# Moving the prompt's group merge into the sample attention of a hybrid decoder step

## The reference, cut to what matters

```
def merge_groups(outs, lses):
    wts = jax.nn.softmax(jnp.stack(lses, 0), axis=0)
    o = jnp.sum(wts[..., None] * jnp.stack(outs, 0), axis=0)
    return o.reshape(o.shape[0], o.shape[1], B_HEADS * HEAD_DIM)

o = jnp.concatenate([o_a, o_b], axis=-1)      # 512 sparse + 256 merged columns
y = jnp.einsum('bte,ed->btd', o, w_out)       # output projection, 768 -> 1024
```

## Time and profile before

| | |
|---|---|
| median of 3 executions | 2952.39 us (2942.93, 2952.39, 2952.66) |
| the profiled execution | 2945.84 us |
| its span, first to last instruction | 2944.0 us |
| mean granted clock of TensorE over the span | 0.946 of 2.4 GHz |
| sample attention | 820.72 to 869.80 us of the span |
| merge | 869.80 to 919.98 |
| output projection, to its last matmul | 919.98 to 997.70 |

### The profile page before, as it was taken

The page is one execution under the profiler, slowest core; times in us unless marked ns, Lnnn a source line. Parts: engine busy times, 40 slices in busy tenths (PEclk is TensorE's granted clock), DMA queues, the critical chain, the costliest instruction groups (busy, mean ns, idle before and its releaser), DMA issues. The chain is left out here.

```text
span 2944.0 us, 39798 instructions
## 1 busy us (share of the span) xinstructions
PE 2691.4 (91%) x15960; PEld 2492.5 (85%) x15960; DVE 1259.2 (43%) x2222; ACT 645.1 (22%) x1148; POOL 959.2 (33%) x466
## 2 busy tenths in 40 slices
PE   6789998778855899999999998996999999999999
PEld 5557877765634899999999997895989999999999
DVE  5157888667725422222222235566342222222222
ACT  4242221546522201000110022345120010001100
POOL 3013440005613533323333344332333333233323
PEclk8889999868966999999999998998999999999999
DMA  4121222524144111111111111223111111111112
GB/s 137 70 59 60 90 77 76 188 69 121 40 140 151 46 49 43 43 43 43 43 43 43 49 43 54 69 91 140 38 38 44 48 45 43 43 43 43 43 43 83
DMA packets 109909, 196.50 MB, mean 67 GB/s; under 512 B 24205, under 2 KB 66317, under 8 KB 109517
## 3 DMA queue, kind: packets, MB, share of 16 engines
q1 hardware_dynamic: 109794, 194.97, 20.7%
HBM read 169.92 MB, written 46.06 MB: 73 GB/s over the span
## 5 line engine op out<-in xcount | busy, mean ns | idle before, releaser
L2014 POOL TENSOR_TENSOR unit_low<-unit_raw,unit_high 128x1024 fp32r<-128x1024 f32 x160 | 450.2, 2814 | 1238.0 <-DVE unit_high L2010 1237.4
L2306 DVE TENSOR_TENSOR x_t<-x_t,m_ps 128x1092 f32<-128x1092 f32 x128 | 165.4, 1292 | 522.9 <-PE m_ps L2027 522.9
L2027 PE MATMUL m_ps<-m_hidden_high,unit_high 128*128 128x364 f32 x1536 | 341.4, 330 | 3.1 <-POOL m_hidden_low L2213 2.9
L2027 PE MATMUL m_ps<-m_hidden_high,unit_low 128*128 128x364 f32 x1536 | 339.6, 329 | 0.0
L2027 PE MATMUL m_ps<-xg_high,unit_high 128*128 128x364 f32 x1536 | 339.3, 329 | 0.0
L2027 PE MATMUL m_ps<-xg_low,unit_high 128*128 128x364 f32 x1536 | 338.8, 328 | 0.0
L2027 PE MATMUL m_ps<-m_hidden_low,unit_high 128*128 128x364 f32 x1536 | 338.4, 328 | 0.0
L2027 PE MATMUL m_ps<-xg_high,unit_low 128*128 128x364 f32 x1536 | 338.0, 328 | 0.0
L2240 ACT ACTIVATE m_relu<-m_ps 128x1092 f32<-128x1092 f32 x64 | 69.4, 1084 | 1210.3 <-PE m_ps L2027 1210.3
L2294 DVE TENSOR_TENSOR m_relu<-m_relu,rstd_all 128x1092 f32<-128x1092 f32 x64 | 83.0, 1296 | 583.5 <-ACT m_relu L2240 583.4
L2027 PEld LDWEIGHTS m_ps<-m_hidden_high,unit_high 128*128 128x128 f32 x1536 | 265.4, 188 | 12.0 <-POOL m_hidden_low L2213 7.9
(11 more groups left out here) (331 smaller groups left out, 3839.9 us busy)
## 6 DMA issues: line engine op xcount, KB each, us to landing
unit_raw<-w_units SPq DMA_DIRECT2D x160, 512.0 KB, 3.5
w_raw<-w_in SPq DMA_DIRECT2D x48, 256.0 KB, 2.9
proj_rows<-rows SPq DMA_DIRECT2D x32, 256.0 KB, 2.0
s_win<-win_cache SPq DMA_DIRECT2D x2, 3968.0 KB
sw_rows<-proj_rows SPq DMA_DIRECT2D x16, 384.0 KB, 3.5
proj_rows<-rows SPq DMA_DIRECT2D x36, 128.0 KB, 1.8
select_work<-xt SPq DMA_DIRECT2D x8, 546.0 KB, 3.7
x_t<-xt SPq DMA_DIRECT2D x4, 1092.0 KB, 11.6
```

Source lines behind the costliest of these rows:

```text
L2014: self.nc.gpsimd.tensor_tensor(self.wl[slot][:, :], self.raw[:, slot, :], self.wh[slot][:, :].bitcast(F32), ALU.subtract).then_inc(self.w_ ...
L2027: last = self.nc.tensor.matmul(ps[:, c, 0:CH], w[wslot][:, wk], v[:, k, c, :], start=(k == 0 and n == 0), stop=(k == nk - 1 and n == 2))
L2306: nc.vector.tensor_tensor(d.x[:, n, :, :], d.x[:, n, :, :], ps[s][:, :, 0:CH], ALU.add).then_inc(d.taken[s], 1)
```

## The change

The merge stage is gone. Its work on the prompt's 8 tiles is now done in the sample attention, one tile a step beside the items; its work on the 64 own rows is done in the output projection.

- **Sparse attention**: after the last page keys, SP loads the window rows of four tiles (`MERGE_FIRST`) into the part of `work` that is free by then.
- **Sample attention**: SP loads a fifth tile ahead of the windows and three behind them. The sums (`merge_below`, `merge_shares`) run for 5 and 3 tiles at a time in steps 1, 2, 6 and 7, the shared products in steps 2 to 9, the adds on POOL, the transposes in steps 4 to 11. ACT copies each turned tile and stores it to `mixed` blocks 4 and 5, and it also stores the items' rows, which are now kept by head (64 outputs, maximum, sum: 66 words). `ob` has 5 buffers instead of 3; the new values have 2 slots instead of 3.
- **Output projection**: SP loads two units, then the own rows (8 + 12 loads), then the parameters and the trunk. ACT's queue loads the six blocks of `mixed`; ACT copies the high parts, DVE makes the low ones. PE makes chunks 1 and 2 (columns 364 on) of the first two units block by block as they come, then turns the own rows, then makes chunk 0, which holds the 64 own columns. The second unit's low part is made by DVE.

The own rows' loads:

```
 class OwnRows:
-    LOADS = AH + NG * BH * 3
+    LOADS = AH + NG * BH
...
+            src = bass.AP(tensor=self.obs.tensor, offset=base + h * (DT * OBW + HD + 2), ap=[[32 * OBW, DB], [OBW, DT], [1, HD + 2]])
+            sp.dma_start(self.b[0:TS, g, h, :], src).then_inc(self.all_in, 16)
```

In `stage_sparse`, on SP, behind the loads of tile j:

```
+                if j == LAST_J - 1:
+                    sp.wait_ge(masked, len([t for t in MASKED if ITEMS[t][0] < LAST_J]))
+                    for n in range(MERGE_FIRST):
+                        smp.load_merge(sp, obp, smp.rows_a[:, n, :, :], n)
```

In `stage_sample`, on SP:

```
+            load_new(1)
+            load_new(0)
+            for n in range(MERGE_FIRST, 5):
+                smp.load_merge(sp, obp, merge_rows(n), n)
             for x, (_, g, i) in enumerate(rest):
                 smp.load_window(sp, a, g, i, kb[x + 2], vb[x + 2], win_in[x + 2])
...
+            for n in range(5, NM):
+                smp.load_merge(sp, obp, merge_rows(n), n)
```

In `stage_sample`, on ACT, at the end of step t:

```
+                n = t - 5
+                if 0 <= n < NM:
+                    act.wait_ge(m_turned, n + 1)
+                    if n >= NMO:
+                        act.wait_ge(m_out[n % NMO], 16 * (n // NMO))
+                    nc.scalar.activation(mt[:, n % NMO, :, :], psx[n % 2][:, 0:2 * P].rearrange("p (k n) -> p k n", k=2), ACT.Copy
+                                         ).then_inc(m_taken, 1)
+                if t >= 3:
+                    store_item(t - 3)
+                if 0 <= n < NM:
+                    store_merge(n)
```

In `stage_sample`, on PE, at the end of step t:

```
+                if t >= 4:
+                    turn_merged(t - 4)
```

In `stage_sample`, on DVE, at the end of step t:

```
+                if t in (1, 6):
+                    merge_below((1, 6).index(t))
+                if t in (2, 7):
+                    merge_shares((2, 7).index(t))
+                if 2 <= t < NM + 2:
+                    merge_rows_of(t - 2)
```

In `stage_out_projection`, on ACT:

```
+            for k in range(NK):
+                act.dma_start(raw[:, k, rows], mixed[k][:, rows]).then_inc(mixed_in[k], 16)
+            for k in range(NK):
+                act.wait_ge(mixed_in[k], 16)
+                nc.scalar.activation(oh[:, k, rows], raw[:, k, rows], ACT.Copy).then_inc(high, 1)
```

In `stage_out_projection`, on PE:

```
+            pe.wait_ge(d.w_low, 2)
+            pe.wait_ge(cleared, 2)
+            for k in range(NK):
+                pe.wait_ge(low, k + 1)
+                for u in range(2):
+                    d.part_product(pe, ps[u], u, k, NK, oth, otl, (1, 2))
+            pe.wait_ge(own.all_in, OWN)
+            pe.wait_ge(merged, 1)
...
+            pe.wait_ge(own_low, 1)
+            for u in range(2):
+                for k in range(NK):
+                    last = d.part_product(pe, ps[u], u, k, NK, oth, otl, (0,))
+                last.then_inc(d.made, 1)
```

More of the change, by code:

```diff
@@ L169, in build_program @@
             otl = c1.enter_context(nc.sbuf_tensor("mixed_low", [P, 6, NCH, CH], F32R))
[L170 to L172 removed]
+            stage_out_projection(nc, a, d, ident, mixed, own, oth, otl)
         stage_mlp(nc, a, d, 0, 0)
@@ L175, in build_program, with released, runs_of @@
         stage_mlp(nc, a, d, 1, 2, o["y_t"])
+def released(nc, known):
+    return sorted(int(s) for s in nc.released_uncleared_semaphores if int(s) not in known)
+def runs_of(numbers):
+    out = []
+    for n in numbers:
+        if out and n == sum(out[-1]):
+            out[-1] = (out[-1][0], out[-1][1] + 1)
+        else:
+            out.append((n, 1))
+    return out
 class Select:
@@ L986, in _ @@
         def _(pool):
-            nc.gpsimd.sem_clear(range(used[0], used[-1] + 1))
+            for first, count in runs_of(used):
+                nc.gpsimd.sem_clear(range(first, first + count))
             nc.gpsimd.memset(pick[:, :, :], 0.0).then_inc(picked, 1)
```

429 lines of the change are left out of this document (228 added, 201 removed).

## The result

The changed kernel takes 2903.35 us (median of 2902.19, 2903.11, 2903.58 and 2909.88) where the kernel before takes 2952.22: the ratio is **0.9852, 95% interval 0.9833 to 0.987**. Timed again on another occasion the ratio was 0.989 (0.9874 to 0.9907): most executions of either kernel fall into two groups some 9 us apart (before 2943 to 2945 and 2952, changed 2902 to 2904 and 2910 to 2913), most likely for a reason that lies ahead of what the change touches (argued at the end); from the lower group to the lower one, and from the upper to the upper, the gain is 40 to 41 us. The prediction was 2908 us, 40.3 us less than before in the profiled execution; profile against profile it is 43.6 us (2945.84 to 2902.19), of which 2.7 us are an earlier start of the sample attention that the change did not make.

What follows compares the result with a forecast made beforehand. No engine bounds the merge stage, a chain of small steps; TensorE, busy 91% of the span, has no gaps in the sample attention at full clock. -0.5, -50.2 and +10.4 give -40.3 us: 2908 us, range 2895 to 2926.

Steps and rivals of the forecast that it cites:

- The sum: Whole kernel: -0.5 us to the next stage's start, -50.2 merge stage, +10.4 output projection, in all -40.3 us; chance 0.63.
- Transposes: Sample attention: two more on TensorE in each of eight steps, 0.5 us a step, 4 us on the path.
- Side work: Sample attention: tiny sums on VectorE and POOL running beside it, 1.5 us added, bounds 0 and 5.
- The lock between VectorE and POOL: Sample attention: VectorE and POOL exclude each other on SBUF; at the rule's worst 5 us paid, without it none.
- ScalarE's queue: Sample attention: stores move to ScalarE at 0.33 us an issue; its step of about 2.2 us stays under TensorE's.
- B: Sample attention: ScalarE's stores bind at 2.11 us an issue, +22 us, 2930 us in all; chance 0.08.
- D: Sample attention: issues hold ScalarE until descriptors are taken; gain eaten at 3.2 us an issue, 2965 us; chance 0.02.
- Rival C: Sample attention: last three tiles to merge land late, VectorE stands in step 6, about 6 us, 2914 us; chance 0.07.
- The projection: Output projection, loading its input and first weights and merging the samples: from 77.7 to 88.1 us.
- Rival A: Output projection: parts late (X+22) or all 72 first products at the low clock (+8.3 us), 2916 us; chance 0.20.
- The step that was wrong: Output projection: the trunk's 4.5 MB behind the own rows need 12 us from X+14, hidden by 4 us.
- The own rows' loads: Output projection: 20 loads at 0.65 us are 13 us of issuing, landed by X+17.

Runs made afterwards that it cites:

- the last kernel: Changed kernel with two unit weights and most own rows loaded in the sample attention, units 2 and 3 before the trunk, own merge woven in, products reordered: 2900.58 us, 0.9842.
- the run with SP: Changed kernel with the stores of sample rows and merged tiles issued by SP again instead of ScalarE: sample attention 46.5 us like for like against 46.7.
- the other order: Changed kernel with TensorE's first products reordered, unit 0 whole and own rows turned before the rest of unit 1: last add at X+91.6, 2.4 us later.
- the run with the early weights: Changed kernel with the first two units' weights loaded in the sample attention, in the page keys' place: last add at X+90.1, 0.9 us later.
- the run with the trunk behind: Changed kernel with TensorE's first products reordered and units 2 and 3 loaded ahead of the trunk: last add at X+87.65, 1.8 us earlier; ratio 0.989.
- the run of all edits: Changed kernel with early unit weights, reordered products, trunk later, own window rows first, merge begun earlier, small exponential behind the copies: 2903.87 us, 0.9868 of the kernel before.

## Why the prediction was right, and what in it was not

- **The sum.** Four stretches make the difference: the sample attention starts 2.7 us earlier (818.01 for 820.72), it lasts 46.74 us for 49.08 (-2.3), the merge stage is gone (-50.2), the projection lasts 89.1 us for 77.7 (+11.4). That is 43.8 us, of which the stages behind give 0.2 back. The first was not predicted and is none of the change's: SP's four loads in the sparse stage are done at 809.8 and the store that ends it comes at 815.27, as predicted, with 5 us between, and among the kernels run here, the same up to that place, the sample attention starts anywhere between 818 and 829. Without it 40.9 us are left, beside 40.3 predicted, and two misses that cancel make it so close: the sample attention ends 1.8 us sooner after its start than forecast, the projection is 1.0 us longer.
- **Transposes** (4 us predicted): sixteen, a pair advancing TensorE by 0.36 us at full clock and more at half of it; its busy time grew by 3.1 us. **Side work** (1.5 us): the three waits, 1.6 us. Together 4.7, against 5.5. By the run without the merge TensorE's last product comes 4.2 us later with it, like for like, and the other 0.6 of the 4.8 us lie behind that product: 3.6 us from it (861.16) to the next load, 3.0 without the merge, and 4.3 in the forecast. (The bound of 0.9 us a step is 7.2 us for eight, not the 6 of the sum's range.)
- **The lock between VectorE and POOL.** Right in kind: VectorE's products with two SBUF inputs grow where they meet POOL's adds, and so does its small copy, which has one input (0.57 us at 853.54, 0.17 without the adds). The rule of the Trainium skill that was weighed there (SBUF — State Buffer, "Who interferes with whom") agrees with the trace: the three products take 1.08 us alone, 1.48 beside POOL, 1.08 again without POOL's adds; and the clearest case is in the last kernels, where VectorE's low part of 1.23 us took 3.24 beside POOL's of 2.72 (the last kernel, timelines of VectorE and POOL, below). Its price was 0.5 us, since only the waits that TensorE sees count.

```profile
868.69 3.24 DVE L2201 TENSOR_TENSOR unit_low<-ss_page_keys,unit_high 128x1024 fp32r<-128x1024 f32 x1
...
868.14 2.72 POOL L2011 TENSOR_TENSOR unit_low<-ss_page_keys,unit_high 128x1024 fp32r<-128x1024 f32 x1 [0.72 <-DVE unit_high L2199]
```

- **ScalarE's queue.** Taken at 0.33 us from SP's row; the medians are 0.33 and 0.38 us, and at 836, where the window loads fill the queues, 0.39. No issue takes more than 0.92 us, where B needs 2.11 and D 3.2: that row refutes both. The second half of their case, that it matters who issues, is refuted by the run with SP.
- **Rival C** was the one with little cover, as said (1.3 us), and the run without early loads shows it at about its price.
- **The projection**, step by step from X, predicted and then measured: the first two weights' landing 6.1 and 6.6, where their casts start at 4.9 and 7.5; TensorE's start 11 and 11.06; the last part 13.4 and 14.5; low parts done 17.7 and 16.8; 72 products done 24.8 and 25.3, with 4.8 us at the low clock for 4.0; chunk 0 starts 26.8 and 27.1; the first unit done 29.8 and 30.5; the third starts 34.2 and 34.9; the end 88.1 and 89.1. Rival A would have shown the low clock for all 72 products or parts at X+22. The start at X+11.06 is right by luck: VectorE's low part of the second unit ended at X+9.8, 0.7 us before its forecast, and its low part of the first block, about 1.2 us, which has to follow and which the sum left out, came on top.
- **The step that was wrong**, without cost to the number: "The trunk's 4.5 MB come behind the own rows and need 12 us from X+14: hidden by 4 us." The trunk is hidden, but I forgot what stands behind it in SP's order: the third unit's weights, which land at X+31.65 and are used at X+31.7. The runs with the early weights and with the other order fell into that: both moved the front of the stage and lost it at once.
- **The own rows' loads** were predicted at 0.65 us an issue and landed at X+17; they took 0.67 and 0.71 and were there at X+17.6. That SP's issuing, and not ScalarE's or the bytes, sets this part of the stage is shown by the run with 44 loads. DMA: Bandwidth & Descriptors of the Trainium skill ("Issuing engines are not separate DMA queues") says that starting DMAs from several engines saves only the sequencer's time, which is usually small beside the transfer. By it nothing is gained on the stores, and the run with SP agrees; for twenty loads of at most 17 KB the sequencer's 14 us are the transfer, and the trace speaks against "small".

## What to carry to other kernels

A stage of small dependent steps (here 50.2 us with TensorE busy for 6) is cheap inside another engine's long stage: 4.8 us. What it then needs is loads that are early and few: rows fetched one stage ahead were worth 5 us, and an order in memory that lets one load fetch what three did was worth 18. Before the front of a stage is made faster, look for what stands last in the same DMA order: a transfer that nobody waits for does not show how little slack it has until its issue and landing are set beside its first use, and two of my edits ran straight into one.

## What the runs showed of the hardware

- The granted clock has its own hand in differences of this size. The stretch 600 to 700 us, in which all these kernels are alike, was granted 0.71 to 0.72 in some executions (before, changed) and 0.62 to 0.65 in others (the run with the early weights, then the run with the trunk behind); the sample attention then starts at 826 to 829 us in the place of 818 to 821. This stretch alone does not order the runs (the run of all edits had 0.66 there and starts at 818.0), but 500 to 800 does for all fourteen traces: 0.83 to 0.85 where the sample attention starts at 818 to 821, 0.82 where it starts at 824.6 (the run without adds), 0.79 or 0.80 where it starts at 826 to 829. That is about the distance between the two groups of times. That it is their cause is not shown, since no execution of the upper group was profiled, of the kernel before or of the changed one. Busy time by stretch of the kernel before, the changed kernel, the run with the early weights and the run with the trunk behind:

```profile
600.00:700.00 100.00, 76.84 (x488) 59.47 (x486) 65.00 (x226) 52.16 (x192) 14.44 (x8) 0.71 0.27 71
```

```profile
600.00:700.00 100.00, 76.59 (x496) 58.60 (x495) 65.12 (x227) 54.09 (x197) 15.84 (x9) 0.72 0.26 69
```

```profile
600.00:700.00 100.00, 79.31 (x464) 61.97 (x463) 60.48 (x219) 49.94 (x186) 10.46 (x7) 0.65 0.26 70
```

```profile
600.00:700.00 100.00, 79.42 (x454) 62.05 (x454) 60.80 (x223) 49.99 (x185) 11.44 (x8) 0.62 0.26 69
```

- The clock can also fall behind a short wait: in the run of all edits together it was 1.00 until 856.56, just behind a wait of 0.52 us, and 0.50 from there to the end of the stage, though TensorE worked without a gap until its last turn at 864.4. Its waits before that, 0.54 and 0.52 us, are like those of the changed kernel (0.31 and 0.52), in which the clock stayed at 1.00. Why it fell is open. Busy time by stretch of that run:

```profile
856.00:857.00 1.00, 0.48 (x3) 0.40 (x3) 1.00 (x3) 1.00 (x5) 0.80 (x2) 0.78 0.05 17
857.00:858.00 1.00, 1.00 (x11) 0.40 (x12) 0.82 (x3) 0.49 (x3) 0.10 (x1) 0.50 0.35 118
```

- An issue of one word for each of 64 rows costs SP as much (0.65 us from one to the next) as one of 64 or 66 words a row (0.67 to 0.71).
